# A fused two-block transformer on one core: the filler products in TensorE's waits are taken out

## The reference, cut to what matters

```
x = first_block(x, ...)     # per layer: mixers (gated MLP, attention, pooling), layer norm,
                            # layer 0: SwiGLU of width 2816; layer 1: top-2 of 8 experts, width 3584
return second_block(x, ...) # per layer: rms norm, sparse attention, retention, convolution,
                            # gates, output product, rms norm, MLP of width 4096

def moe_ffn(x, router_w, w1, w3, w2):
    logits = (xt @ router_w).astype(F32)
    top_v, top_i = lax.top_k(logits, TOP_K)
    top_w = jax.nn.softmax(top_v, axis=-1)
    ...
    for e in range(N_EXPERTS):
        y = y + gates[:, e:e + 1].astype(x.dtype) * swiglu(xt, w1[e], w3[e], w2[e])
```

## Time and profile before

| | |
|---|---|
| time, three runs | 2458.58, 2465.29, 2465.87 us, median 2465.29 |
| span of the profiled execution | 2455.5 us (its own time outside the profile is not given) |
| TensorE busy | 2422.5 us, 99% |
| its weight loads | 2004.6 us, 82% |
| VectorE, ScalarE busy | 1962.4 us (80%), 1452.9 us (59%) |
| mean granted TensorE clock | 0.996 of full |
| read from HBM | 623.06 MB, 254 GB/s over the span |

### The profile page before, as it was taken

How to read it: one execution, slowest core, us unless ns; L and a number is a source line. 1 busy time by engine, 2 the same in 40 slices (tenths; PEclk the granted TensorE clock), 3 DMA queues, 4 the chain that set the end, 5 groups by cost and what they waited for, 6 DMA issues and landing times.

```text
span 2455.5 us, 29832 instructions
## 1 busy us (share of the span) xinstructions
PE 2422.5 (99%) x11599; PEld 2004.6 (82%) x11599; DVE 1962.4 (80%) x2459; ACT 1452.9 (59%) x1506; POOL 31.7 (1%) x44
## 2 busy tenths in 40 slices
PE   9999999999999999999999999899999999999998
PEld 7788877888888888888888888788888888888887
DVE  5855668999899988898989898799875568997645
ACT  4344443777777777777777777356545445654543
POOL 0000001000000000000000000000000000000000
PEclk9999999999999999999999999999999999999999
DMA  8366454999999999999999998553556656445653
GB/s 278 102 224 185 158 172 143 334 351 362 373 353 345 361 374 354 346 361 374 355 344 362 374 354 311 173 168 123 176 179 190 188 180 201 125 157 178 195 194 121
DMA packets 274155, 626.17 MB, mean 255 GB/s; under 512 B 17899, under 2 KB 27255, under 8 KB 273880
## 3 DMA queue, kind: packets, MB, share of 16 engines
q1 hardware_dynamic: 271708, 615.92, 72.1%
q0 software_dynamic: 1872, 6.82, 0.8%
q10 hardware_dynamic: 428, 1.45, 0.2%
HBM read 623.06 MB, written 1.07 MB: 254 GB/s over the span
## 4 chain that ended last, share of the span: by engine, by line
PE 96%; DVE 2%; issue 1%; ACT 0%; DMA 0%; POOL 0%; POOLq 0%; ACTq 0%; DVEq 0%
PE tile L779 29%; PE tile L781 28%; PE tile L780 28%; PE aux L902 4%; PE aux L1195 1%; PE aux L1414 1%; PE aux L1326 1%; DVE units_parts L2011 0%; PE aux L1339 0%; PE aux L1338 0%; PE aux L1215 0%; PE aux L1216 0%; PE aux L1103 0%; PE aux L1471 0%; PE aux L1012 0%
## 5 line engine op out<-in xcount | busy, mean ns | idle before, releaser
L2011 DVE TENSOR_TENSOR units_parts<-units,high 128x1024 fp32r<-128x1024 f32 (+3 forms) x369 | 551.7, 1511 | 89.5 <-ACT high L1542 84.2
L1542 ACT ACTIVATE high<-units 128x1024 fp32r<-128x1024 f32 (+3 forms) x369 | 470.3, 1290 | 174.4 <-PE tile L781 72.3
L780 PE MATMUL tile<-units_parts,acts 128*128 128x512 f32 (+2 forms) x1456 | 558.2, 383 | 0.0
L779 PE MATMUL tile<-high,acts 128*128 128x512 f32 (+2 forms) x1068 | 422.6, 396 | 5.9 <-DVE units_parts L2011 3.2
L781 PE MATMUL tile<-high,acts 128*128 128x512 f32 (+2 forms) x1068 | 411.4, 385 | 0.0
L780 PEld LDWEIGHTS tile<-units_parts,acts 128*128 128x128 f32 x1456 | 274.9, 189 | 51.3 <-issue 1.2
L780 PE MATMUL tile<-units_parts,zbuf_parts 128*128 128x512 f32 x616 | 239.8, 389 | 0.0
L779 PEld LDWEIGHTS tile<-high,acts 128*128 128x128 f32 x1068 | 201.3, 188 | 45.6 <-DVE units_parts L2011 5.3
L781 PEld LDWEIGHTS tile<-high,acts 128*128 128x128 f32 x1068 | 201.0, 188 | 40.9
L781 PE MATMUL tile<-high,zbuf_parts 128*128 128x512 f32 x508 | 197.9, 390 | 0.0
L779 PE MATMUL tile<-high,zbuf_parts 128*128 128x512 f32 x436 | 171.1, 392 | 0.0
(11 more groups left out here) (435 smaller groups left out, 4970.9 us busy)
## 6 DMA issues: line engine op xcount, KB each, us to landing
units<-in_moe_w SPq DMA_DIRECT2D x216, 1024.0 KB, 5.3
units<-in_w_in SPq DMA_DIRECT2D x134, 512.0 KB, 3.8
units<-in_w_ff SPq DMA_DIRECT2D x128, 512.0 KB, 3.6
q_buf<-in_moe_w SPq DMA_DIRECT2D x54, 1024.0 KB, 5.4
k_buf<-in_moe_w SPq DMA_DIRECT2D x54, 1024.0 KB, 5.5
nat<-in_moe_w SPq DMA_DIRECT2D x54, 1024.0 KB, 5.2
units<-in_ffn_w SPq DMA_DIRECT2D x48, 512.0 KB, 3.6
units<-in_w_out SPq DMA_DIRECT2D x32, 512.0 KB, 3.3
```

The source lines that it names most:

```text
L779: nc.tensor.matmul(bank, lhs[0], high, start=start, stop=False)
L780: nc.tensor.matmul(bank, lhs[0], low, start=False, stop=False)
L1542: nc.scalar.activation(high_slot(SG[0], n) if wide_ else high_slot(SG[0], n)[:, 0:cols], halves(weights) if wide_ else weights[:, 0:cols], ...
L2011: V.tensor_tensor(low, weights, high, ALU.subtract).then_inc(SG[0].low_ready, 1)
```

## The change

The function `keep_busy` and its calls are taken out. Nothing takes their place; where a filler carried a wait, the next real product carries it.

```
-            def keep_busy(times, tile=0, width=2 * P):
-
-
-                if tile in freed:
-                    pe.wait_ge(*freed[tile])
-                for _ in range(times):
-                    nc.tensor.matmul(tiles[tile][:, 0:width], ident, consts[:, 0:width], start=True, stop=True)
...
                     turned_at[src is x, stage, 0] = C.aux.n
-                    for h in range(2):
-                        turn_half(src, 0, h, stage)
-                        keep_busy(3 + h)
+                    turn_block(src, 0, stage)
...
                     for b in range(TB):
-                        keep_busy(5 - 2 * b, 0, P)
                         pe.wait_ge(x_loaded[b], 16)
...
-                    keep_busy(4, sums_at[-1])
                     pe.wait_ge(router_ready, 1)
                     turned_at[True, 4, 1] = C.aux.n
-                    keep_busy(1, sums_at[-1])
                     turn_half(x, 1, 0, 4)
...
                     route(bank, 1, 1).then_inc(S.aux_full, 1)
-                    keep_busy(2)
                     pe.wait_ge(rank_parts, 2)
...
                     mm.then_inc(S.aux_full, 1)
-                    keep_busy(3)
...
             scatter()
-            keep_busy(9)
```

## The result

| | before | after |
|---|---|---|
| time, ten runs of each: median | 2460.35 us | 2467.47 us |
| lowest, highest | 2454.75, 2465.95 | 2463.67, 2475.82 |
| ratio after / before | | 1.0035, 95% interval 1.0023 to 1.0046 |
| span of the profiled execution | 2455.5 us | 2462.7 us |
| mean granted clock in it | 0.996 | 0.990 |

The ten runs of the kernel before include the three of the forecast. The change costs 7 to 9 us: the medians are 7.1 us apart, the means (2461.1 and 2468.8 us) 7.7, the profiled executions 7.2, and the ratio makes it 8.6 (interval 5.7 to 11.3). The profiled execution of the changed kernel took 2464.51 us with a span of 2462.7, so 1.8 us lie around a span, not the 9.8 that I worked with.

What follows compares the result with a forecast made beforehand. TensorE's own order of work was taken to bound the kernel (busy 2422.5 of 2455.5 us). Low-clock terms 2.0 + 1.5 + 2.2 + 0.6 = 6.3 us, added to 2463.2, gave 2469.5 us; range 2461.5 to 2477.

Steps and rivals of the forecast that it cites:

- the 9.8 that I worked with: Whole execution: 9.8 us lie around the 2455.5 us span, taken from the runs' median of 2465.3 us.
- No time given back directly: Entry, routing, block 2: removing the fillers' own time gains 0, with -1.0 us kept as an end at the entry.
- Entry, 2.0: First products at 11.63, after 2.94 us of idle: low clock costs 2.0 us, ends 0 and 3.0.
- Router's chain, 1.5: Routing, 8 transposes and 32 router products behind a 3.9 us idle: low clock costs 1.5 us, ends 0 and 4.8.
- the short stretch: Router's chain: a low stretch of 3.3 us, priced at 1.5 us, part of a stretch falling in the idle time.
- the end of 4.8: Router's chain: all 40 short operations at the low clock would cost 4.8 us more.
- That rival: Router's chain and gather: clock stays low under the router's 24 products; all places together 12.2 us, 2475.4 us; chance 0.15.
- Gather, 2.2: Gather at 433.32, after 4.6 us, the longest idle: near certain low clock costs 2.2 us, ends 1.0 and 3.0.
- Block 2, 0.6: Block 2's first products: low clock costs 2.2 us, the 1.65 us wait for `nat` takes that much, leaving 0.6.
- The expert stage absorbs nothing: Expert stage: TensorE is never idle (1106.00 us), so every microsecond lost at the entry and in the routing counts in full.
- To the whole: Whole time: 6.3 us added to the three runs' mean of 2463.2, not their median, gives 2469.5 us.
- The idle of 8.8 to 11.6 at 1.00: Entry, ahead of the first products: clock stays at 1.00, a sign that not every wait lowers it; entry's term might be none.

Runs made afterwards that it cites:

- experiment 5: Kernel before with all 34 fillers kept in place with their waits, but 8 columns wide; ratio 1.0024, mean 6.6 us over the kernel before.
- experiment 2: Kernel before without the fillers of both entries (8 and 16 products), the routing's kept; ratio 1.0014, mean 3.4 us over the kernel before.
- experiment 7: Kernel before without only the eight fillers ahead of the input's transposes at the entry; ratio 0.9991, mean 2462.2 us beside 2463.2.
- experiment 3: Kernel before without only the five fillers ahead of the router's transposes; ratio 1.0025, mean 7.0 us over the kernel before.
- experiment 4: Kernel before without only the fillers between the router's products and the gather (2 and 3); ratio 1.0009, mean 2.3 us over the kernel before.
- experiment 6: Kernel before without only the 16 fillers at the entry of block 2; ratio 0.9998, mean 0.9 us under the kernel before.
- experiment 1: Kernel before without only the ten fillers of the routing, those of both entries kept; ratio 1.0022, mean 2465.7 us, 5.7 us over the kernel before.

## Why the prediction was right, and where its steps were not

It forecast +6.3 us by the loss of clock in TensorE's waits; +7.2 us was measured in the profile, 7.1 in the medians and 7.7 in the means. The predicted 2469.5 us stands against a median of 2467.47 and a mean of 2468.8. The mechanism is shown: experiment 5 keeps everything of the fillers but their work and has the changed kernel's time.

That the sum came so near is in part luck. The router's chain cost 2.1 us more than its term, while entry, gather and block 2 together cost 1.8 us less than theirs (the profile pair gives 1.5 + 3.6 + 1.7 - 0.2 = 6.7 for the four), and a level 2.1 us too high (2463.2 against a mean of 2461.1 in ten runs) made up for a loss forecast 1.4 us too small. The steps:

- **No time given back directly.** Right: the first product is at 11.67 against 11.63, and the 16 transposes took 3.65 us against 3.9 worked out. In block 2 the first product came 0.2 us sooner behind the scatter (13.02 against 13.23), the rest went by VectorE as assumed.
- **Entry, 2.0.** Measured 1.54 in the profile pair. Not as I had it, though: the clock was up when the products began and fell 1.3 us later, at 12.9; in experiments 2 and 5 it was low from the first product. As a mean over executions it is open (experiment 7).
- **Router's chain, 1.5.** The term that was mis-sized: 3.6 us (2.52 to 6.15). I took the short stretch because part of it would fall into the idle time; the clock stayed down through the whole chain, the case for which I had the end of 4.8 and a rival. The lengths that I priced with, 3.3 and 6.7 us, were all that I had read in the kernel before (a third stretch there, 375.7 to 379.1, is as short); the routing's is 16.9 us. That rival's place and its point of decision, the clock low under the 24 router products, came true, its 12.2 us did not.
- **Gather, 2.2.** Measured 1.7 (6.15 to 7.87). But "the longest idle of all" was not what made it slow: in the changed kernel the clock had been down since 426.0, and experiment 3 has the slow gather with its fillers in place. The wait alone can do it too (experiment 4). The first expert products, which I had expected to be low, were at the high level: the clock came back in the gather.
- **Block 2, 0.6.** Measured nothing (7.91 to 7.70), and experiment 6 agrees. Some ten slow products fitted into the 1.65 us wait, with 0.19 to spare; I had counted 0.6 beyond it.
- **Not foreseen:** 0.9 us more between 16.40 and the routing. The changed kernel has two low stretches in the attention (367.9 to 371.3 and 378.1 to 381.6), the kernel before one (375.7 to 379.1). The change has no filler there, and experiments 4 and 6, with the fillers that stand ahead of it, have two as well: I take it for the execution, not the change.
- **The expert stage absorbs nothing.** Right: 7.87 in, 7.91 out.
- **To the whole.** Adding to the mean of the three runs (2463.2) rather than to their median (2465.3) was nearer, but still too high: ten runs have a mean of 2461.1, 35 later ones 2460.0. The 9.8 us around the span was wrong, 1.8 in truth.
- **The idle of 8.8 to 11.6 at 1.00** was read as a sign that a wait may do no harm. The changed kernel's 8.9 to 11.6 is at 1.00 too, and its clock fell at 12.9: the level printed for a wait does not tell what follows it. Nor does the level printed for the first microseconds: for 12.0 to 17.0 in experiment 2 the view has 1.00, with products 0.43 us apart. There the distance of starts decides.

What the Trainium skill says in "TensorE: Matmul & The Clock Gate", section "Why this matters for your kernels", on waits between bursts of products, the trace agrees with where a wait is long (3.75 to 4.05 us ahead of the router's transposes and of the scatter), and shows more: at 427.1 in experiment 2 the clock fell while TensorE worked.

## What to carry to other kernels

Where TensorE waits for a chain of small steps, ask what runs behind the wait: a low clock costs what TensorE itself bounds (a router's chain, a gather, the first products of a long stage), and little or nothing where another engine sets the pace (0.6 us and less at block 2). Price a fall of the clock as lasting through the whole chain of short work behind it, not as one short stretch, and expect it in some executions and not in others: compare means of ten and more runs with their mean clocks. Filling the waits fuller gained 4 to 6 us of 2460 here, mostly because the long times no longer occur; which of the waits the gain comes from was not settled.

## What the runs showed of the hardware

- The clock can fall while TensorE is busy, some microseconds behind a short idle, and not come back in 13.5 us of unbroken work of 128 and 256 columns, with five products of 8 (experiment 2, 427.1 to 440.6).
- In all six profiles whose routing is low, the clock came back within the gather, 2.0 us (experiment 3) to 6.0 us (experiment 1) after its start, and in none of the five with a low router chain under the router's 24 products, which took 5.4 us.
- The same program took from 2452.9 to 2470.5 us in 94 runs on three chips, and within each chip's runs the time goes with the mean granted clock at a correlation of -0.92 to -0.96. The seven runs with all the added fillers lie within 4.3 us; the 24 of the kernel before beside them within 15.2.
